# Conformer's projection first in the mixer, parts of VectorE's work at other pieces, and constant matrix products in TensorE's pauses

## The reference, cut to what matters

```python
for l in range(2):
    h = rmsnorm(x, attn_norm[l])
    x = x + hybrid_mixer(h, ...)        # h @ w_in, four branches, gates, w_branch, w_out
    h = rmsnorm(x, ffn_norm[l])
    x = x + (swiglu(h) if l == 0 else moe_swiglu(h))     # moe: the top 2 of 8 experts per token

# hybrid_mixer: proj = h @ w_in holds the gates and the inputs of four branches
# A gMLP:      u * (causal(w_s) @ layernorm(v) + b_s)
# B attention: q, k normalized and rotated, softmax, values
# C latent attention: latents c_q, c_kv normalized, multiplied up to q, k, v; q, k normalized and rotated
# D Conformer: z = a * sigmoid(g); z = causal depthwise conv of 31 taps (z) + bias; silu(layernorm(z))
# mix = (sum_n sigmoid(gate_n) * (branch_n @ w_branch[n])) @ w_out
```

## Time and profile before

| what | us |
|---|---|
| median of 3 runs | 1124.6 (1124.08 to 1124.77) |
| the profiled execution | 1124.35 |
| its span, from the first to the last instruction | 1122.6 |
| PE busy | 1064.7 (95%) |
| DVE busy | 838.5 (75%) |
| ACT busy | 646.7 (58%) |
| mean granted clock of TensorE | 0.984 |

### The profile page before, as it was taken

One profiled execution on the slowest core, in us unless ns is written; L12 is line 12 of the kernel. 1 busy time (PEld: TensorE's weight loads), 2 busy tenths in 40 slices (PEclk: granted clock), 3 DMA queues, 4 the chain that ended last, 5 costly groups with the idle time before them and its releaser, 6 DMA issues.

```text
span 1122.6 us, 15778 instructions
## 1 busy us (share of the span) xinstructions
PE 1064.7 (95%) x5632; PEld 910.9 (81%) x5632; DVE 838.5 (75%) x1178; ACT 646.7 (58%) x904; POOL 29.0 (3%) x76
## 2 busy tenths in 40 slices
PE   5999999999999999999899969999999999999997
PEld 4888777889999998888687857888787878788886
DVE  4579888654545447579898565988889898989895
ACT  4667545443434336456545345666767676667664
POOL 6000000030000000000000000000000000000000
PEclk9999989999999999999999988999999999999999
DMA  9554445675455454444345374899898989898981
GB/s 264 178 169 150 150 132 180 210 205 187 152 187 174 169 195 156 152 160 160 125 155 198 119 258 146 292 326 334 297 342 290 357 286 357 289 350 300 353 296 58
DMA packets 125324, 248.64 MB, mean 221 GB/s; under 512 B 4912, under 2 KB 50034, under 8 KB 125280
## 3 DMA queue, kind: packets, MB, share of 16 engines
q1 hardware_dynamic: 123136, 243.02, 63.4%
q0 software_dynamic: 2144, 5.03, 1.9%
HBM read 246.99 MB, written 1.05 MB: 221 GB/s over the span
## 4 chain that ended last, share of the span: by engine, by line
PE 74%; DVE 18%; ACT 5%; issue 2%; DMA 1%; ACTq 0%; DVEq 0%; POOL 0%; POOLq 0%
PE bank L349 22%; PE bank L351 21%; PE bank L350 21%; DVE wlo L337 8%; ACT whi L330 3%; PE bank L899 2%; PE bank L898 2%; PE bank L957 1%; DVE h L1355 1%; DVE dacc L1560 1%; PE bank L612 1%; DVE x L1353 1%; DVE h L1492 1%; DMA gain<-in_attn_norm 1%; PE bank L919 1%
## 5 line engine op out<-in xcount | busy, mean ns | idle before, releaser
L337 DVE TENSOR_TENSOR wlo<-ring,whi 128x1024 fp32r<-128x1024 f32 (+3 forms) x506 | 541.1, 1120 | 108.3 <-ACT whi L330 107.4
L349 PE MATMUL bank<-whi,hTh 128*128 128x512 f32 (+3 forms) x1328 | 479.3, 361 | 11.4 <-DVE wlo L337 8.8
L330 ACT CAST whi<-ring 128x1024 fp32r<-128x1024 f32 (+3 forms) x506 | 457.1, 972 | 30.1 <-PE bank L351 17.6
L351 PE MATMUL bank<-whi,hTl 128*128 128x512 f32 (+3 forms) x1328 | 469.2, 353 | 0.0
L350 PE MATMUL bank<-wlo,hTh 128*128 128x512 f32 (+3 forms) x1328 | 469.1, 353 | 0.0
L349 PEld LDWEIGHTS bank<-whi,hTh 128*128 128x128 f32 x1328 | 252.4, 190 | 51.6 <-DVE wlo L337 15.7
L351 PEld LDWEIGHTS bank<-whi,hTl 128*128 128x128 f32 x1328 | 252.2, 190 | 30.6
L350 PEld LDWEIGHTS bank<-wlo,hTh 128*128 128x128 f32 x1328 | 252.5, 190 | 28.3 <-issue 0.5
L349 PE MATMUL bank<-whi,oTh 128*128 128x512 f32 x128 | 53.2, 415 | 4.0 <-DVE oTl L1666 4.0
L1678 DVE SCALAR_TENSOR_TENSOR act<-bank,rstd,sig 128x256 f32<-128x256 f32 x22 | 9.6, 479 | 57.9 <-ACT sig L1209 57.9
L350 PE MATMUL bank<-wlo,oTh 128*128 128x512 f32 x128 | 51.7, 404 | 0.0
(11 more groups left out here) (299 smaller groups left out, 877.7 us busy)
## 6 DMA issues: line engine op xcount, KB each, us to landing
ring<-in_w_in SPq DMA_DIRECT2D x40, 1024.0 KB, 5.2
ring<-in_moe_w_down SPq DMA_DIRECT2D x40, 1024.0 KB, 6.0
ring<-in_moe_w_gate SPq DMA_DIRECT2D x32, 1024.0 KB, 7.2
ring<-in_moe_w_up SPq DMA_DIRECT2D x32, 1024.0 KB, 7.3
ring<-in_moe_w_gate SPq DMA_DIRECT2D x16, 768.0 KB, 6.1
ring<-in_moe_w_up SPq DMA_DIRECT2D x16, 768.0 KB, 4.5
ring<-in_ffn_w_gate SPq DMA_DIRECT2D x11, 1024.0 KB, 5.3
ring<-in_ffn_w_up SPq DMA_DIRECT2D x11, 1024.0 KB, 5.4
```

The source lines that it names most:

```text
L330: nc.scalar.copy(whi[pc.part(hf)][:, 0:n], pc.raw[:, hf * n:(hf + 1) * n]).then_inc(hi_done, 1)
L337: nc.vector.tensor_tensor(wlo[q][:, 0:n], pc.raw[:, hf * n:(hf + 1) * n], whi[q][:, 0:n].bitcast(F32), ALU.subtract).then_inc(lo_done, 1)
L349: nc.tensor.matmul(o, sh, wh, start=start, stop=False)
L351: return nc.tensor.matmul(o, sl, wh, start=False, stop=stop)
```

## The change

The chunk of the Conformer (D) becomes the first one. Everything that the chunks' order entails is renumbered: which chunk is evicted at which step, and for which value of `prj_ev` its readers wait. `glu` moves from step 10 to 2, and `d_zT` from 11 to 3 (now into bank 5), with ACT's copy to `zpad`. A's and C's steps come one to three steps later; `o_lower(l, 0, 6)` moves from step 8 to 10. In `c_qkT` the wait for `o_lo[0]` stands ahead of the keys instead of the queries.

On DVE the taps are distributed anew; 26 of the 62 now lie at steps 4 to 6. `c_rotate_qk` moves from step 7 to the start of step 9, ahead of the split of piece 11. `softmax_start(l, 0)` moves from 10 to 11. `d_center` and `d_finish` move to 25 and 26, one and two steps earlier, and the last product of D becomes a function of its own, `d_gate`, at 27.

PE gets `idle_products(n)`: n products of two constant 128x128 float32 tiles into bank 3, which nobody reads. They stand ahead of and behind `transposed_h(0)` (12 and 10), ahead of the router's logits (7), ahead of the ranks (10), behind them (9), and behind `gather(0)` (6).

```diff
-CHUNKS = [(C_Q, 352), (A_U, 512), (B_Q, 384), (B_Q + 384, 384), (D_A, 512)]
+CHUNKS = [(D_A, 512), (C_Q, 352), (A_U, 512), (B_Q, 384), (B_Q + 384, 384)]
@@ PE
+            def idle_products(n):
+                for _ in range(n):
+                    nc.tensor.matmul(bank[3][:, 0:P], ident[:, :], upper[:, :], start=True, stop=True)
             def c_latent_T(l):
                 pe.wait_ge(cn_ready, l + 1)
+                pe.wait_ge(zpad_ready, l + 1)
             def c_qkT(l):
                 pe.wait_ge(cqk_ready, l + 1)
                 pe.wait_ge(az_ev, l + 1)
-                pe.wait_ge(o_lo[0], l + 1)
                 for w, src in enumerate((ctq, kc)):
+                    if w:
+                        pe.wait_ge(o_lo[0], l + 1)
             def d_zT(l):
+                pe.wait_ge(hT_lo, 8 * l + 4)
                 pe.wait_ge(glu_ready, l + 1)
-                pe.wait_ge(sc_ev, 8 * l + 4)
...
-                        last = nc.tensor.transpose(bank[6][:, T * c + P * m:T * c + P * (m + 1)],
+                        last = nc.tensor.transpose(bank[5][:, T * c + P * m:T * c + P * (m + 1)],
@@ PE, small(s)
                     if s == 3:
+                        d_zT(l)
+                    if s == 5:
                         c_latent_T(l)
-                    if s == 4:
+                    if s == 6:
                         c_up(l)
-                    if s == 6:
+                    if s == 7:
                         a_z(l)
-                    if s == 8:
+                    if s == 9:
                         a_oT(l)
-                    if s == 9:
+                    if s == 10:
                         c_qkT(l)
-                    if s == 10:
+                    if s == 11:
                         scores(l, 0)
-                    if s == 11:
-                        d_zT(l)
+                    if s == 13:
                         b_qkT(l)
...
+                    if s == 25:
+                        d_mean(l, dacc, conv_ready, dmean_mm, 6)
                     if s == 26:
-                        d_mean(l, dacc, conv_ready, dmean_mm, 6)
-                    if s == 27:
                         d_mean(l, zpad[:, :, 0:T], dsq_ready, dvar_mm, 7)
@@ PE, router and start
             def router():
+                idle_products(7)
                 pe.wait_ge(hT_lo, 16)
...
+                idle_products(10)
                 pe.wait_ge(member_ready, 1)
...
+                idle_products(9)
...
             pe.wait_ge(const_ready, 1)
+            idle_products(12)
             transposed_h(0)
+            idle_products(10)
             mixer(0)
...
             gather(0)
+            idle_products(6)
@@ ACT, mixer
                     if s == 1:
                         chunk_ev(0)
+                    if s == 3:
+                        chunk_ev(1)
                         square_latents()
+                        act_e.wait_ge(zT_mm, l + 1)
+                        nc.scalar.copy(zpad[:, :, D_CONV - 1:D_CONV - 1 + T],
+                                       bank[5][:, :].rearrange("p (c t) -> p c t", t=T)).then_inc(zpad_ready, 1)
...
# roots of C at 4 (was 2), cT at 5 (3), chunk_ev(2) at 5, root of A and up_evict at 6 (4),
# chunk_ev(3) and the root of q, k at 7 (5), chunk_ev(4), B's squares and o_upper at 9 (8),
# root of B and the copies of C's q, k at 10 (9), the copies of B's q, k at 13 (11)
@@ DVE, mixer
-                taps = {13: (0, 8), 14: (8, 4), 16: (12, 6), 17: (18, 2), 19: (20, 10), 20: (30, 8), 22: (38, 10),
-                        23: (48, 10), 25: (58, 4)}
+                taps = {4: (0, 4), 5: (4, 10), 6: (14, 12), 13: (26, 4), 14: (30, 4), 16: (34, 8), 20: (42, 4),
+                        22: (46, 8), 23: (54, 8)}
                 for s in range(MIX_PIECES):
+                    if s == 9:
+                        c_rotate_qk(l)
                     if s + 2 < MIX_PIECES:
                         split_lo(dve, pcs[s + 2], piece_half(s + 2))
...
                     if s == 2:
-                        c_norm_latents(l)
+                        glu(l)
                         prep(l)
                     if s == 4:
+                        c_norm_latents(l)
+                    if s == 6:
                         a_norm(l)
-                    if s == 5:
+                    if s == 7:
                         c_sum_qk(l)
-                    if s == 6:
+                    if s == 8:
+                        a_gate(l)
                         c_scale_qk(l)
-                    if s == 7:
-                        a_gate(l)
-                        c_rotate_qk(l)
-                    if s == 8:
+                    if s == 10:
                         o_lower(l, 0, 6)
-                    if s == 9:
                         b_sum_qk(l)
-                    if s == 10:
                         b_rotate_qk(l)
-                        glu(l)
+                    if s == 11:
                         softmax_start(l, 0)
...
+                    if s == 27:
+                        d_gate(l)
...
+                    if s == 25:
+                        d_center(l)
                     if s == 26:
-                        d_center(l)
-                    if s == 28:
                         d_finish(l)
```

More of the change, by code:

```diff
@@ L1073, in chunk_ev @@
                         b = bank[2 * (ci % 2) + m]
-                        w = BW if ci == 4 else n
+                        w = BW if ci == 0 else n
                         last = nc.scalar.mul(prj[:, m, c0:c0 + w], b[:, 0:w], rstd[:, 1, m:m + 1])
-                    if ci == 4:
+                    if ci == 0:
                         for m in range(MT):
@@ L1083, in square_latents @@
                     lat = prj[:, :, C_Q:C_Q + 320]
-                    act_e.wait_ge(prj_ev, n_chunk * l + 1)
+                    act_e.wait_ge(prj_ev, n_chunk * l + 2)
                     nc.scalar.activation(scr0[:, 0:640].rearrange("p (m c) -> p m c", m=MT), lat,
@@ L1124, in mixer @@
                         chunk_ev(0)
+                    if s == 3:
+                        chunk_ev(1)
                         square_latents()
-                    if s == 2:
+                        act_e.wait_ge(zT_mm, l + 1)
+                        nc.scalar.copy(zpad[:, :, D_CONV - 1:D_CONV - 1 + T],
+                                       bank[5][:, :].rearrange("p (c t) -> p c t", t=T)).then_inc(zpad_ready, 1)
+                    if s == 4:
                         act_e.wait_ge(cms, l + 1)
@@ L1130, in mixer @@
                                              scale=1.0 / CKV).then_inc(cms_root, 1)
-                    if s == 3:
-                        chunk_ev(1)
+                    if s == 5:
                         act_e.wait_ge(cnT_mm, l + 1)
@@ L1135, in mixer @@
                         nc.scalar.copy(cT[0:CQ - P, 2, :], bank[5][0:CQ - P, 0:T]).then_inc(cnT_ev, 1)
-                    if s == 4:
+                        chunk_ev(2)
+                    if s == 6:
                         act_e.wait_ge(ams, l + 1)
@@ L1140, in mixer @@
                         up_evict()
-                    if s == 5:
-                        chunk_ev(2)
+                    if s == 7:
+                        chunk_ev(3)
                         act_e.wait_ge(qms, l + 1)
@@ L1145, in mixer @@
                                              scale=1.0 / C_QK).then_inc(qms_root, 1)
-                    if s == 7:
-                        chunk_ev(3)
-                    if s == 8:
-                        act_e.wait_ge(prj_ev, n_chunk * l + 4)
+                    if s == 9:
+                        chunk_ev(4)
+                        act_e.wait_ge(prj_ev, n_chunk * l + 5)
                         nc.scalar.activation(ym[:, :, 0:512], prj[:, :, B_Q:B_Q + 512], ACT.Square).then_inc(b_sq, 1)
                         o_upper(l, 0, 6)
-                    if s == 9:
+                    if s == 10:
                         act_e.wait_ge(bms, l + 1)
@@ L1155, in mixer @@
                                              scale=1.0 / HD).then_inc(bms_root, 1)
-                        chunk_ev(4)
                         for w in range(2):
@@ L1164, in mixer @@
                         gate_ev(0)
-                        act_e.wait_ge(zT_mm, l + 1)
-                        nc.scalar.copy(zpad[:, :, D_CONV - 1:D_CONV - 1 + T],
-                                       bank[6][:, :].rearrange("p (c t) -> p c t", t=T)).then_inc(zpad_ready, 1)
+                    if s == 12:
+                        attention_exp(l, 0, 0)
+                    if s == 13:
+                        attention_exp(l, 0, 1)
                         act_e.wait_ge(sc_mm, 8 * l + 4)
@@ L1513, in a_norm @@
             def a_norm(l):
-                dve.wait_ge(prj_ev, n_chunk * l + 2)
+                dve.wait_ge(prj_ev, n_chunk * l + 3)
                 for m in range(MT):
@@ L1543, in glu @@
             def glu(l):
-                dve.wait_ge(prj_ev, n_chunk * l + 5)
+                dve.wait_ge(prj_ev, n_chunk * l + 1)
```

(2 more changed lines are left out.)

17 lines of the change are left out of this document (6 added, 11 removed).

## The result

The changed kernel takes 1109.4 us (median; 1107.4 to 1110.0), the kernel before on the same chip 1124.7 (1124.1 to 1125.0): a ratio of 0.986 (0.985 to 0.988), 15.2 us faster. The forecast was 1105.6 with a range from 1096.5 to 1113: the direction and the account of the waits were right, the terms for the start and for the router's clock were not. The gain was put at 18.7 us and came out at 14.5 in the profiled execution, which took 1109.89 with a span of 1108.1.

A forecast was written before the change was run, and what follows sets the result against it. PE's work was taken as the bound, so only pauses and half rate could go: 28.7 us of gains less 10.0 of new costs, 18.7, taking 1124.35 to 1105.6, with a range of 1096.5 to 1113.

The forecast's parts named there:

- the account of the waits: Both mixers: PE's waits for probabilities, D's output, queries and Conformer input, 14.9 us in all, would go, less new waits.
- Taps covered at steps 4 to 6: Mixers: DVE finishes the 26 moved taps, 10.3 us, before it is needed, with 0.6 us to spare.
- The two rests of 0.3 and 0.2 per mixer: Second half of each mixer: what remains of the probabilities' wait (0.3 us) and of D's output wait (0.2 us).
- The new wait for the keys: At the keys' transposes: PE waits 2.8 us for `o_lo[0]`, 5.6 us in both mixers.
- `d_zT` waiting 1.1 in the first mixer: At step 3, first mixer alone: PE waits 1.1 us behind `glu`, with bounds 0 to 2.7.
- The start: Before and at the first weights: full rate gains 2.0 us, starting later costs 0.3 (0 to 1.2).
- Because the products leave no pause over 1.5 us, I take full rate: Router: constant products fill its pauses, so the gather and the first 12 matmuls behind it gain 6.0 us.
- the clock at 0.50 in the gather: Router's gather: a listed sign of a wrong forecast; a right one meant 32 matmuls in 3.5 us.
- the 5.8: Router and experts: 6.0 us from full rate, with 0.2 given back for ACT's split of the fourth piece.
- The rival "the router stays at half rate": Router: pauses still drop the clock and 6.0 us is lost, giving 1111.6, or 1116.6 with overhanging products; chance 0.17.
- Half rate, 0.9 expected behind each keys' wait: Behind the keys' wait: a fall of the clock costs up to 1.7 us; 0.9 taken each, 1.8 in all.

The follow-up runs named there:

- e3_old_taps: The changed kernel with the convolution's taps where they were before, except the last four, at step 23 instead of 25: 1118.9 us, ratio 0.995.
- e4_o_lower_early: The changed kernel with `o_lower` at step 9, ahead of DVE's splits of pieces 11 and 12: 1100.1 us, ratio 0.979.
- e6_start20: `e4_o_lower_early` with 20 instead of 10 constant products ahead of the first weights: 1099.9 us, ratio 0.979.
- e8_changed_again: The changed kernel measured once more without any edit: 1108.3 us, ratio 0.986.
- e10_all: `e4_o_lower_early` with products at later norms, 20 at the start, 14 behind the ranks, ACT's first square sum before its piece 1 split: 1097.7 us.
- e5_keys_wait_first: The changed kernel with `c_qkT` waiting for `o_lo[0]` ahead of the queries again, as before the change: 1115.8 us, ratio 0.990.
- e1_no_products: The changed kernel with all constant products left out: 1112.8 us, ratio 0.989.
- e2: The kernel before the change with only the 54 constant products added at the same places: 1118.7 us, ratio 0.995.
- e7_gain_first: `e4_o_lower_early` with the gain's DMA issued ahead of the positions' on POOL: 1100.1 us, ratio 0.977.

## Why the prediction was right, and where it was off

- **Taps covered at steps 4 to 6: right.** PE never waited for a `wlo` at pieces 6 to 9. DVE ended the taps at 64.7, 4.6 us behind the end of `c_up` (X = 60.10; 4.7 counted), and stood idle for 0.71 us before it was needed (0.6 counted):
```profile
59.87 4.83 DVE L1574 SCALAR_TENSOR_TENSOR dacc<-zpad,cw,dacc 128x256 f32<-128x256 f32 x12
65.41 1.83 DVE L337 TENSOR_TENSOR wlo<-ring,whi 128x768 fp32r<-128x768 f32 x2 [0.71 <-ACT whi L330]
```
The waits of the earlier trace rows went, and `e3_old_taps` brings back the 4.3. The two rests of 0.3 and 0.2 per mixer measured 0; a wait of 0.3 for the gate's `gsig` stands there instead.
- **The new wait for the keys: right**, 2.8 forecast, 2.82 measured, in both mixers and in both profiles. DVE's count to the end of `o_lower` (X+24.6) gives 84.70; PE's keys began at 84.74. The two splits (3.5 counted) and `o_lower` on DVE:
```profile
80.53 3.56 DVE L337 TENSOR_TENSOR wlo<-ring,whi 128x1024 fp32r<-128x1024 f32 x4
84.01 0.68 DVE L1523 TENSOR_TENSOR oTl<-bank,oTh 128x512 fp32r<-128x512 f32 x1
```
The stations before fit as well (`cqk_ready` counted at 80.5, the split behind it began at 80.53), so this is not errors that cancel. It was the sum's largest loss, and `e4_o_lower_early` removes it.
- **`d_zT` waiting 1.1 in the first mixer: failed, a wait that did not come.** `glu` was counted to end at 37.7 and ended at 38.4:
```profile
37.76 0.69 DVE L1558 TENSOR_TENSOR dxc<-prj 128x512 f32<-128x512 f32 x1
```
PE arrived only at 39.2, later by its start, by half rate there and by its own work. The last of these is enough to hide the wait: in `e6_start20` and `e8_changed_again`, whose starts held, PE still reached `d_zT` at 37.68 and 37.72, not at the counted 36.6, behind a `glu` that ended at 37.5 and 37.4. In `e6_start20` its first two pieces took 11.0 us, not 10.6, and the third began 0.4 later, behind its `wlo`. Only `e10_all` shows such a wait, of 0.40.
- **The start: failed, 2.3 us.** "The 15 matmuls would take 2.3 us instead of 4.3" and "I take 0.3 us later": a gain of 1.7. Measured, the first weights came 0.9 later, within the forecast's bounds of 0 to 1.2, and up to 1.7 stayed at half rate, which was in no bound: a loss of 0.6. Larger first pieces in front held the gain vector back: DVE's first `h`, which waits for it, began at 10.07 instead of 9.41, and at 9.87 to 10.55 in all nine profiles with these pieces and the old order of issues on POOL, against 9.41 and 9.56 in the two with the small ones. The Trainium skill's rule, that transfers of different engines interleave on the same 16 DMA engines ("DMA: Bandwidth & Descriptors", Issuing engines are not separate DMA queues), which the forecast left out of its sum, agrees with this. The first piece landed at 11.3 instead of 9.45. ACT's timeline at the second piece:
```profile
19.19 1.99 ACT L330 CAST whi<-ring 128x1024 fp32r<-128x1024 f32 x2 [1.96 <-DMA ring<-in_w_in]
```
It landed at 19.17; before, at 13.7. PE at the start of the changed kernel:
```profile
11.10 2.19 PE L531 MATMUL bank<-ident,h 128*128 128x128 f32 x16
13.12 2.40 PE L523 MATMUL bank<-upper,ident 128*128 128x128 f32 x20
18.06 0.50 PE L349 MATMUL bank<-whi,hTh 128*128 128x512 f32 x1 [2.54 <-DVE wlo L337]
```
The first products did raise the clock (16 transposes in 2.2 us), but the ten behind ended at 15.5 and left a pause of 2.5 us, and at 18.4 the clock fell. I had counted what the clock costs and not the pause that is left before the first weights. `e6_start20` fills it and the start holds; with the pause it holds only at times (two of eight profiles).
- **"Because the products leave no pause over 1.5 us, I take full rate": failed in the first profile, 3.6 us.** By the forecast's own list, the clock at 0.50 in the gather is a sign of its being wrong. The pauses were as short as counted, and the clock fell all the same, inside the gather:
```profile
654.29 2.25 PE L523 MATMUL bank<-upper,ident 128*128 128x128 f32 x18
657.66 0.33 PE L907 MATMUL bank<-pick,htokh 128*128 128x128 f32 x1 [1.11 <-DVE wcol L1852]
662.38 2.87 PE L523 MATMUL bank<-upper,ident 128*128 128x128 f32 x12
664.90 0.77 PE L349 MATMUL bank<-whi,hTh 128*128 128x512 f32 x1
```
One pause of 1.11 us, then 21 of the gather's matmuls at full rate (the 2.40 us stretch above), then 0.50; the last six products took 2.5 us instead of 1.3. So the router kept 2.2 of the 5.8. In `e8_changed_again` and in seven of the eight other kernels with the products the gather held and nearly all of it came (the exception is `e5_keys_wait_first`, half rate from 666.9). The rival "the router stays at half rate" thus came in part, in some executions.
- **Half rate, 0.9 expected behind each keys' wait: right as a mean.** None in one profile, 1.7 at both in the other, and in `e1_no_products` and `e3_old_taps`, with the same 2.8 us wait, in the second mixer alone: four falls behind eight waits. Instead the second mixer's first piece fell at 431.4 in the first profile, a place for which the sum had no term.

Of the 4.2 us between the two gains, the start took 2.3 and the router 3.6; the wait at `d_zT` that did not come (1.1) and the lower cost behind the keys, 1.8 against the 1.7 at 431.4, go the other way or even out, as do the rests of 0.3 and 0.2 (1.0 in both mixers, less 0.6 of the gate). -2.3 - 3.6 + 1.1 + 0.1 + 0.4 is -4.3.

## What to carry to other kernels

- Price moved work by counting the engine's queue up to the instruction that someone waits for: this gave the new wait to 0.02 us, and the remedy with it (the one short instruction on which PE waits goes ahead of two splits that nobody yet needs).
- Constant products are worth what half rate costs behind the pauses that they fill. Those that reached up to the next real matmul kept the clock up wherever this was tried; those that left a pause did so only at times. Look for the pause behind the last of them, and for the place where they become the wait themselves.
- Where falls of the clock decide over 1 to 5 us, forecast a spread for the kernel and not one number, and don't explain a difference of that size from one profile.

## What the runs showed of the hardware

- Falls of TensorE's clock do not repeat from execution to execution of one kernel: behind the same 2.8 us wait the granted clock was 1.00 in one profile of the changed kernel and 0.50 in the next. Over the twelve profiles:

| pause of PE | fell | seen |
|---|---|---|
| 4.3 us, probabilities (before, `e2`, `e3`) | 6 | 6 |
| 3.8 us, keys (`e5`) | 2 | 2 |
| 2.8 us, keys (changed, `e8`, `e1`, `e3`) | 4 | 8 |
| 2.1 to 2.6 us, start, ten products ahead of it | 6 | 8 |
| 2.0 us, D's output (before, `e2`) | 2 | 4 |
| 1.1 us, ahead of the gather's short matmuls | 2 | 9 |
| up to 0.7 us, turns between stages, no products | 4 | 20 |

- A fall cost 1.2 to 1.7 us where PE is busy throughout. The feed-forward took 200.4 us with one (`e7_gain_first`) and 198.9 without, the second mixer 206.8 (`e6_start20`) and 205.3 (`e4_o_lower_early`), the first mixer 206.9 with one at its start and 205.7 without.
- A product of two 128x128 float32 tiles took 0.22 us at full rate and about 0.43 at half, both in the products' own rows (twenty took 4.63 us and ten 2.40; six in the router took 2.5), as the forecast had taken them from other instructions.
- With 320 KB more in each of the first two transfers of one queue, a transfer of 512 KB issued by another engine (the gain) landed 0.66 us later.
